# A two-layer trunk with memory attention on one core: layer 0's attention interleaved with halves of projections, norms taken from PSUM

## The reference

```python
for i in range(DEPTH):                       # DEPTH = 2
    mem_kv = rmsnorm(mem, g_mem[i]) @ w_mem_kv[i]          # 1024 -> 2048
    mem_k, mem_v = halves of mem_kv as (256, 4 heads, 256)
    h = rmsnorm(x, g_mix[i])
    if i == 0:
        x = x + swa_mixer(h, mem_k, mem_v, ...)     # q 1024, k 128, v 128, xq 1024; out 2048 -> 1024
        x = x + swiglu(rmsnorm(x, g_ffn[0]), ...)   # 1024 -> 2816 -> 1024
    else:
        x = x + ssd_mixer(h, mem_k, mem_v, ...)     # state space scan, conv, gated norm; out 3072 -> 1024
        x = x + moe_swiglu(rmsnorm(x, g_ffn[1]), ...)  # 8 experts, top 2
return rmsnorm(x, g_final)
```

## Time and profile before

| | us |
|---|---|
| median of 3 runs | 1753.18 |
| lowest and highest | 1750.74, 1760.78 |
| the profiled execution, its span | 1750.7 |
| PE busy | 1577.2 (90%) |
| DVE busy | 1139.1 (65%) |
| ACT busy | 948.9 (54%) |
| POOL busy | 57.0 (3%) |
| HBM read | 390.91 MB, 224 GB/s over the span |

### The profile page before, as it was taken

The page is one execution under the profiler, slowest core; times in us unless marked ns, Lnnn a source line. Parts: engine busy times, 40 slices in busy tenths (PEclk is TensorE's granted clock), DMA queues, the critical chain, the costliest instruction groups (busy, mean ns, idle before and its releaser), DMA issues.

```text
span 1750.7 us, 22451 instructions
## 1 busy us (share of the span) xinstructions
PE 1577.2 (90%) x8652; PEld 1365.5 (78%) x8652; DVE 1139.1 (65%) x999; ACT 948.9 (54%) x907; POOL 57.0 (3%) x75
## 2 busy tenths in 40 slices
PE   5996689999989886897949999999999999999996
PEld 4995569899978885675848878888888888888884
DVE  5335354544543665644448878788897879889885
ACT  4424534433443643243336776777777677777763
POOL 1000000000000001700000000000000000000000
PEclk9999889999998897997969999999999999999998
DMA  7540035455552332042438989999999999999992
GB/s 257 192 145 1 25 138 186 158 187 178 189 171 84 110 121 96 1 145 84 166 135 315 349 321 330 346 331 368 326 350 322 341 355 325 375 327 352 332 347 100
DMA packets 229857, 392.92 MB, mean 224 GB/s; under 512 B 7280, under 2 KB 82208, under 8 KB 229792
## 3 DMA queue, kind: packets, MB, share of 16 engines
q1 hardware_dynamic: 229792, 392.01, 64.1%
HBM read 390.91 MB, written 1.07 MB: 224 GB/s over the span
## 4 chain that ended last, share of the span: by engine, by line
PE 71%; DVE 11%; ACT 6%; issue 6%; DMA 4%; SPq 1%; POOL 0%; DVEq 0%; ACTq 0%; POOLq 0%
PE PB L1205 21%; PE PB L1206 21%; PE PB L1207 21%; DMA y<-in_moe_w_down 2%; DVE cv L985 2%; ACT whi L478 2%; DMA ring<-in_moe_w_gate 1%; PE PB L1529 1%; PE PB L1506 1%; DVE wlo L783 1%; DVE xn_lo L789 1%; ACT whi L483 1%; DVE nt L819 1%; PE PB L1457 1%; DVE nt L1009 1%
## 5 line engine op out<-in xcount | busy, mean ns | idle before, releaser
L783 DVE TENSOR_TENSOR wlo<-ring,whi 128x2048 fp32r<-128x2048 f32 (+1 forms) x103 | 234.1, 2275 | 292.7 <-PE PB L1207 263.5
L1205 PE MATMUL PB<-whi,cat_hi 128*128 128x512 f32 (+1 forms) x1048 | 404.4, 386 | 18.9 <-DVE cat_lo L1155 9.9
L1207 PE MATMUL PB<-whi,cat_lo 128*128 128x512 f32 (+1 forms) x1048 | 399.1, 381 | 0.0
L483 ACT ACTIVATE whi<-ring 128x2048 fp32r<-128x2048 f32 x168 | 321.0, 1916 | 138.8 <-PE PB L1207 118.5
L1206 PE MATMUL PB<-wlo,cat_hi 128*128 128x512 f32 (+1 forms) x824 | 310.3, 377 | 0.0
L789 DVE TENSOR_TENSOR wlo<-ring,whi 128x2048 fp32r<-128x2048 f32 x112 | 255.4, 2287 | 68.4 <-ACT whi L483 68.3
L478 ACT ACTIVATE whi<-ring 128x2048 fp32r<-128x2048 f32 (+1 forms) x103 | 195.4, 1898 | 107.6 <-PE PB L1207 98.0
L1205 PEld LDWEIGHTS PB<-whi,cat_hi 128*128 128x128 f32 x1048 | 200.1, 191 | 56.6 <-DVE wlo L789 10.1
L1207 PEld LDWEIGHTS PB<-whi,cat_lo 128*128 128x128 f32 x1048 | 200.1, 191 | 37.8
L1205 PE MATMUL PB<-hT_hi,whi 128*128 128x256 f32 x744 | 217.5, 292 | 6.6 <-DVE hT_lo L810 6.6
L1206 PE MATMUL PB<-hT_lo,whi 128*128 128x256 f32 x744 | 215.3, 289 | 0.0
(11 more groups left out here) (247 smaller groups left out, 2219.4 us busy)
## 6 DMA issues: line engine op xcount, KB each, us to landing
ring<-in_moe_w_gate SPq DMA_DIRECT2D x64, 1024.0 KB, 6.4
ring<-in_moe_w_up SPq DMA_DIRECT2D x64, 1024.0 KB, 7.2
y<-in_moe_w_down SPq DMA_DIRECT2D x48, 1024.0 KB, 7.9
ring<-in_moe_w_down SPq DMA_DIRECT2D x40, 1024.0 KB, 5.2
ring<-in_ssm_w_in SPq DMA_DIRECT2D x24, 1024.0 KB, 5.3
y<-in_moe_w_up SPq DMA_DIRECT2D x24, 1024.0 KB, 8.1
y<-in_moe_w_gate SPq DMA_DIRECT2D x24, 1024.0 KB, 6.2
ring<-in_w_mem_kv SPq DMA_DIRECT2D x16, 1024.0 KB, 5.7
```

The lines of the kernel that those rows point to most:

```text
L483: nc.scalar.activation(ehi[slot(m)], eraw[slot(m)], ACT.Copy).then_inc(q["hi_ready"], 1)
L783: ve.tensor_tensor(wlo[:, n % LOS, 0:w], ring[:, n % RING, 0:w], whi[:, n % HIS, 0:w].bitcast(F32), ALU.subtract).then_inc(q["lo_ready"], 1)
L1205: mm(out, lhs[0], rhs[0], start=start, stop=False)
L1207: return mm(out, lhs[1], rhs[0], start=False, stop=stop)
```

## The change

Six things.

1. The list of units has a new order: k/v unit, `q`, `xq0`, `k0`, `v0`, `out0` (now alternating its two column halves), `k1`, the feed-forward, and only then `v1`, the memory values of layer 1. SP loads `x` and the constants first, `mem` after the first unit.
2. PE's attention loop covers all 20 steps. Between `scores`/`values` of a step and its `transpose_probs` stands half a unit (`filler`), and after the transposes of every second step, and of each of the last four, another: the 12 units of `xq0`, `k0`, `v0` and the first 4 of `out0`, 32 halves in all. ACT and DVE have the splits and drains of those units between their own steps.
3. The memory's normed rows are kept in `xnm` and used for both layers; the second load of `mem`, its squares and its scaling are gone. Its transposes for layer 1 stand between parts of `out0`, those of the norm before the feed-forward between units of `k1`, those of layer 1's norm between units of `v1`.
4. In all norms a group is now two 128-row blocks by all 256 tokens. ACT writes the high part straight from PSUM with the gain as its scale (`norm_hi`), DVE the low part from PSUM in one `scalar_tensor_tensor` (`norm_lo`). The product `nt` is gone. PE's transposes now wait until both row tiles are scaled.
5. Sums of squares are taken in parts of 512 columns, each as soon as its part of `x` or `y` is there (all norms but the first two); POOL adds them up. DVE adds the first row tile to `x` when that tile's matmuls are done (`row_full`), not the whole unit's.
6. The output is stored in two halves.

```diff
-    units = []
-    for layer in range(2):
...
+    units = [(cols(sw, 256 * j, 256), "a") for j in (4, 0, 1, 2, 3, 5, 6, 7, 8)]
+    units += [(cols(mk0, 256 * j, 256), "a") for j in range(4)]
+    units += [(kb(mk0, kg, 2 + n), "b") for n in range(2) for kg in range(2)]
+    units += [(kb(a["swa_w_out"][0], kg, n), "b") for kg in range(4) for n in range(2)]
+    units += [(cols(mk1, 256 * j, 256), "a") for j in range(4)]
...
     units += ffn
+    units += [(kb(mk1, kg, 2 + n), "b") for n in range(2) for kg in range(2)]
...
+        def units_before(step):
+            return (step + step // 2) // 2 if step <= 16 else step - 4
...
-            sp.wait_ge(q["final"], 2)
-            sp.dma_start(out[0].rearrange("(t p) d -> p t d", p=P), xn[:, :, :]).then_inc(q["stores"], 16)
-            sp.wait_ge(q["stores"], 16)
+            for t in range(NT):
+                sp.wait_ge(q["final"], t + 1)
+                sp.dma_start(out[0][P * t:P * t + P, :], xn[:, t, :]).then_inc(q["stores"], 16)
+            sp.wait_ge(q["stores"], 32)
...
+            def square_part(r, src, t, n, width):
+                c = square_at(r, t, n)
+                ac.wait_ge(q["sq_done"], c)
+                nc.scalar.activation(actf[:, c % 2, :], src[:, t, 512 * n:512 * n + 512], ACT.Square, scale=width ** -0.5,
+                                     accum_out=ssq[:, c:c + 1]).then_inc(q["sq_done"], 1)
+            def norm_hi(r, g0, dst, groups):
+                for g in groups:
+                    f = TR_BEFORE[r] + g
+                    ac.wait_ge(q["tr_full"], f + 1)
+                    for i in range(2):
+                        k = 2 * g + i
+                        last = nc.scalar.activation(dst[:, k, :], PB[4 + f % 2][:, S * i:S * i + S], ACT.Identity, scale=pc[:, g0 + k:g0 + k + 1])
+                    last.then_inc(q["t_hi"], 1)
...
+            exp_step(0, True)
+            for s in range(20):
+                if s + 1 < 20:
+                    exp_step(s + 1, s + 1 < 16)
+                if s:
+                    cat_hi_step(s - 1, 8 + 2 * (s - 17))
+                ahead(XQ0 + units_before(s) + 2)
+                for u in range(units_before(s - 1) if s else 0, units_before(s)):
+                    if u < 4:
+                        xq_out("xq0", u)
+                    elif u < 8:
+                        k_out("k0", u - 4)
+                    elif u < 12 and u % 2:
+                        v_out("v0", (u - 8) // 2)
+                probT_step(s, s < 16)
...
-            ahead(L1 + 2)
-            ac.wait_ge(q["y_drained"], 1)
-            square_sum(R_H1, x, dump)
-            norm_hi(R_H1, hT_hi, KD)
-            cross_q(1)
+            ahead(V1 + 1)
+            for t in range(NT):
+                for n in range(2):
+                    ac.wait_ge(q["y_drained"], 2 * t + n + 1)
+                    square_part(R_H1, x, t, n, D)
+            ahead(V1 + 2)
+            norm_hi(R_H1, PC_MIX + 8, hT_hi, range(2))
+            ahead(V1 + 3)
+            v_out("v1", 0)
+            norm_hi(R_H1, PC_MIX + 8, hT_hi, range(2, 4))
...
+            def norm_lo(r, g0, dst, groups):
+                for g in groups:
+                    f = TR_BEFORE[r] + g
+                    ve.wait_ge(q["t_hi"], f + 1)
+                    for i in range(2):
+                        k = 2 * g + i
+                        last = ve.scalar_tensor_tensor(out=dst[1][:, k, :], in0=PB[4 + f % 2][:, S * i:S * i + S], scalar=pc[:, g0 + k:g0 + k + 1],
+                                                       in1=dst[0][:, k, :].bitcast(F32), op0=ALU.mult, op1=ALU.subtract)
+                    last.then_inc(q["t_lo"], 1)
...
+            scores(0, True)
+            half = 0
+            for s in range(20):
...
+                if s + 1 < 20:
+                    scores(s + 1, s + 1 < 16)
...
+                if s:
+                    values(s - 1, s - 1 < 16)
...
+                filler(half)
+                half += 1
+                transpose_probs(s, s < 16)
+                if s % 2 or s >= 16:
+                    filler(half)
+                    half += 1
...
             for j in range(4):
-                gemm_a_fill(13 + j, fills["xq0"] + j, hT)
...
+                gemm_a_fill(K1 + j, fills["k1"] + j, memT1)
+                if j < 2:
+                    transposed(R_F0, xn, range(2 * j, 2 * j + 2))
...
-            pe.wait_ge(q["y_drained"], 1)
-            transposed(R_H1, xn, D)
+            for j in range(2):
+                for kg in range(2):
+                    for t in range(NT):
+                        gemm_b_part(V1 + 2 * j + kg, fills["v1"] + 2 * j, kg, 2, t, memT1)
+                    if j == 0:
+                        transposed(R_H1, xn, range(2 * kg, 2 * kg + 2))
```

More of the change, by code:

```diff
@@ L769, in _ @@
             expert(last_job, True)
[L770 to L771 removed]
+            for t in range(NT):
+                for n in range(2):
+                    ac.wait_ge(q["sc_done"], 4 * last_job + (5 + 2 * t + n))
+                    square_part(R_FIN, x, t, n, D)
         @block.vector
@@ L1249, in gemm_b @@
+            def gemm_b(n, f, kgs, actT, full=False):
                 for kg in range(kgs):
[L1250 to L1251 removed]
                     for t in range(NT):
[L1253 to L1257 removed]
@@ L1258, in gemm_b @@
-                    last.then_inc(q["units_used"], 1)
-            def memory_kv(layer, n, m):
-                for j in range(4):
-                    gemm_a_fill(n + j, fills[f"k{layer}"] + j, m)
-                for j in range(2):
-                    gemm_b(n + 4 + 2 * j, fills[f"v{layer}"] + 2 * j, 2, m)
+                        gemm_b_part(n + kg, f, kg, kgs, t, actT, full and kg == kgs - 1)
             def scores(s, swa):
@@ new lines, in _ @@
+            values(19, False)
+            transposed(R_MEM1, xnm, range(2))
+            pe.wait_ge(q["cat_done"], 18)
+            for kg in range(2, 4):
+                if kg == 3:
+                    pe.wait_ge(q["cat_done"], 20)
+                for n in range(2):
+                    for t in range(NT):
+                        gemm_b_part(OUT0 + 2 * kg + n, fills["out0"] + 2 * n, kg, 4, t, cat, kg == 3)
+                    if kg == 2 and n == 0:
+                        transposed(R_MEM1, xnm, range(2, 4))
```

505 lines of the change are left out of this document (265 added, 240 removed).

## The result

| | us |
|---|---|
| kernel before, median (lowest, highest) | 1755.81 (1750.74, 1760.78), 4 runs |
| changed kernel, median (lowest, highest) | 1680.2 (1675.9, 1684.94), 4 runs |
| ratio, 95% interval | 0.9568 [0.9536, 0.9599] |
| profiled execution after, its span | 1678.7 (before 1750.7) |

The changed kernel is 4.3% faster.

A forecast was written before the change was run, and what follows sets the result against it. PE was taken as the bound, idle only in attention and four norms. Terms for start, attention, norms, clock and end sum to 79.6 us off 1750.7: 1671.1, forecast 1671 us, range 1660 to 1697.

The forecast's parts named there:

- start: Before the first projection matmul: `x` loaded first brings it from 28.69 to 20.7 us, gain 8.0 (ends 4 and 11).
- rest up to the feed-forward: Memory's transposes -2.2, attention 35.4, second memory's norm 8.4, clock behind it 3.1, norm before the feed-forward 4.1 us.
- clock in the feed-forward: Feed-forward: 186.6 us of work took 188.5, so 1.9 us of clock come back.
- norm of layer 1, first unit behind it: Behind the feed-forward: units of `memV` cover the norm, gain 12.6 us; first unit at better clock, gain 2.7.
- gated norm: Norm at 791.03 us: transposes start no earlier, groups go from 1.38 to about 1.25 us each, gain 1.1.
- norm before the experts: Two squares of 1.06 us become one part of about 0.8, an add moves earlier: gain 1.5 (ends 0 and 2.5).
- experts: Expert stage: 816 us unchanged; rival that it takes the gain back, 1748 us, chance 0.03.
- end: Final scaling and store: first row scaled during second's reduction, 2.3 us, plus half store 0.7; gain 3.0.
- Attention: Attention stage: halves of units cover PE's waits, 56.5 us instead of 91.9, gain 35.4; chain-stays rival 1695 us, chance 0.12.
- the prediction's step formula: Attention: PE's work alone is 8 x (2.98 - 1.39) + 8 x (4.56 - 1.48) + 4 x 3.97 = 53.2 us.
- the rival: Interleaved attention stage: PSUM-bank cycling keeps PE at the lower clock, 1817 us if throughout; chance 0.02.
- The bound of -1.5: Gated norm: lower end of its gain of 1.1 us; the upper end was 3.

The follow-up runs named there:

- Two cheap edits: Kernel before, with DVE scaling `prob` ahead of the next maximum and both attention loops joined, cross queries drained earlier: 1731.26 us, ratio 0.9885.
- two more edits: Changed kernel with four gated-norm banks, plus reordered additions and last square, and row scaling before the first expert's low part: 1667.3 us, ratio 0.9512.

## Why the prediction was right, and where it wasn't

The time lay 9 us above the forecast and in its range; faster had 0.95. By the profiles 7.6 us of the forecast gain are missing: 3.85 in the experts, which were chance, 2.1 in the logits, 1.9 at the gated norm and 1.2 in the clock of the feed-forward, against 1.0 more than forecast at the start and as much up to the feed-forward. By its own terms (gain forecast, gain measured):

| step | forecast | measured |
|---|---|---|
| start | 8.0 | 9.0 |
| rest up to the feed-forward | 48.8 | 49.8 |
| clock in the feed-forward | 1.9 | 0.7 |
| norm of layer 1, first unit behind it | 15.3 | 15.0 |
| gated norm | 1.1 | -0.8 |
| norm before the experts | 1.5 | 1.7 |
| logits | 0 | -2.1 |
| experts | 0 | -3.85 |
| end | 3.0 | 3.0 |

(The small rest, about 0.5 us, lies in layer 1's projections. The second line: the feed-forward started at 248.49 instead of 329.10, less four units of `v1`, 21.8 us, which moved behind it, and less the start.)

**Attention: right size, half a reason.** The step read "they stand where PE waited 1.4 us, so if the chain does not grow, it is covered". It is covered: 54.9 us (56.5 forecast), and with DVE's old order 53.4, so the halves suffice, with the fault in DVE's queue and without it, and the number is no luck. But the prediction took the wait in the earlier trace rows for the length of the chain. It was to a large part the place of one operation in DVE's queue: with that operation moved, the waits for `prob` fell from 21.7 to 1.9 us, though 7 us came back on others. The earlier trace rows even shows it: 162.25, the exponential of step s+1, ends its wait by `nm` of s+1, and the scaling of s comes after it (162.73). A second part was one wait for `xqT` of 6.1 us, which the prediction's step formula removed without a word: its periods add up to 76.2 us (8 x 2.98 + 8 x 4.56 + 4 x 3.97), the stage was 91.9, and the 15.7 between them, the seam above all, stand nowhere in the prediction. Two cheap edits would have given 24 of the 37 us. The same argument, turned round, failed in the run without halves: it expected 37 us lost, and the attention lost 13.9.

**Start: right size, a part of the reason.** The gain was 9.0 us of 8.0 forecast. The prediction put it down to `x` coming first and named late tables only as an end of the term. By the rows of the run with the old load order about half of it are the tables, for which the kernel before had waited 6.66 us.

**Clock in the attention: the rival was rightly small.** It is 1.00 in 144 us of interleaved work. The prediction read the 0.94 of the kernel before as the clock of steps in which PE waits; in these steps it was 1.00, and the 0.94 came from the seam. The Trainium skill's "psum-queue depth-cycling" (TensorE: Matmul & The Clock Gate) was not seen here, neither with PE waiting in each step (1.00 from 128.98 to 190 us) nor with the halves going over banks 0 to 3 (1.00).

**The gated norm: a wrong sign.** The step was "1.38 together; now two of 0.485 ... and a bank's round trip ... about 1.25. Gain 1.1". The gain in the groups came out nearly so, 0.85 us (13.53 to 12.68), though both paces were longer than taken: the new one is 1.48 us a group, since the chain of transposes, high part and low part at the low clock is longer than the forecast took. What failed is the sentence before it, "the transposes now wait for both rows, so they start no earlier", which priced that wait at nothing. It costs 2.0 us by the run with norms from PSUM alone, of which squares in parts gave back only 0.4 (10.35 to 9.96), since POOL and a split of ACT stand in between. The bound of -1.5 held it.

**The logits: a term that was missing.** The prediction had no term for the clock in the stages behind a hole that it changed; here that was 2.1 us. It is not chance: nine profiles show 10.79 or 10.80 us, all of kernels with norms in the new groups; three with the old groups show 8.5 to 8.7, and two with the new 8.11 and 8.61.

**The experts** were right as forecast, no change; the 3.85 us are the spread of single executions.

Open: why the clock in the logits is 0.50 in some kernels and 0.64 to 0.68 in others. The hole in front is not the reason: 12.03 us with 10.79, 12.04 with 8.11, 9.41 with 10.79. Some parts of the change were not undone by themselves either: the reuse of the memory's normed rows, whose stage is simply absent, the squares in parts, the earlier add of the first row, and the output in two halves.

## What to carry to other kernels

When an engine waits in every step of a loop, first read the helper's own queue row by row: if the idle time stands in front of an operation of the *next* step, the order is at fault, and swapping two lines may give what a reordering of the whole program gives. Do that alone before interleaving other work, because cover hides the fault and takes its credit. Where transposes wait for a bank, more banks are cheap: here a few edited lines gave 4 us in the hole and 5 more by the clock behind it. Do not count on such a gain of clock when you add edits up: with two more edits in front of the same stages 4 of these 5 us were gone again.

## What the hardware showed that I had not expected

- An addition of POOL on 128x1 takes 0.22 to 0.28 us alone, (spans on POOL are rough in the profile), but 1.31 when it starts at 721.55, 0.06 us behind a scaling of DVE (721.49 to 722.78); it ends at 722.86. In the run with the other order of additions one took 1.73 us beside the end of DVE's 2.29 us low part and the product behind it, and `rstd` 1.41 instead of 0.57 beside the scaling. This agrees with the Trainium skill (SBUF — State Buffer, "🔬 SBUF: two separate sides"): DVE and GpSimd share a port pair that is held for a whole instruction, and the loser blocks; the page says this of DVE operations in a 2-port mode or with two SBUF inputs. Whether the scaling ran in such a mode no run here shows. A tiny operation of POOL in a critical chain should not meet a long one of DVE.
- The clock behind a hole of PE does not follow its length. First 11 us behind it: 0.77 (hole 22.65 us), 0.86 (21.01), 1.00 (18.59), but 0.85 (17.08). The same holds for the logits, as said above. The runs don't show why.
